# An expert's 96 rows loaded as 128 pieces of three quarters of a row, in a decoder block with 32 experts

## Chip, cores and metric

The kernel runs on one core of a Trainium2 chip, in one launch. The metric is the device time of one execution in microseconds. All tensors are float32.

## What is computed

One layer of a decoder on 1,024 tokens of 1,024 features. First come three token mixers side by side (a recurrent one, a chunked one, sliding-window attention), their gated sum and an output projection. Then comes the part that the change touches, a mixture of 32 experts of which each token uses two:

```
h = rms_norm(x, norm2_g) * (1 + sc2) + sh2
group = top-1 of softmax(h @ w_rg)              # 4 groups of 8 experts
expert 1, 2 = top-2 of softmax(h @ w_re) within the group; weights = their shares
for each expert e, on the rows of its tokens:
    gate, up = split(rows @ w_e_in[e])          # 1024 x 1024
    y = (silu(gate) * up) @ w_e_out[e]          # 512 x 1024
x = x + gt2 * (sum of each token's two y, by weight)
```

## The kernel before

The engines each run a program of their own and meet at semaphores. Only the part from the output projection on matters here.

**Router and scatter.** The output projection goes over 8 tiles of 128 tokens. For each tile VectorE (DVE) finds the two experts of a token and its rank among the tokens of that expert, and from them a place: row 96 * e + rank of a table `x_slots` in DRAM (`CAP` is 96). This is `L2262` to `L2266`; `L2266` writes the places as integers. GpSimd (POOL, `L725`) scatters the normalized rows of the tile there, once for the first and once for the second expert. Ranks of 96 and more are sent out of bounds, and handled in extra blocks of their own.

**Experts.** Then 32 experts follow, each with up to 96 rows. The work of one:

- ACT's queue loads the rows to `e_xs[s]` (`load_x`, `L1700`), two buffers in turn. The load takes 128 rows of the table, 96 of this expert and 32 of the next.
- DVE transposes them (`turn_x`, `L2386`): 12 turns of 32 partitions x 256 columns in blocks of 32 x 32, into `e_xT[s]`. ACT scales and shifts the result (`modulate`, `L1717`). Expert 0 is transposed on TensorE (PE) in place of that (`L1288`).
- PE multiplies by `w_e_in` in two halves (`step`), ACT takes the silu (`L1725`), DVE the product (`activate`, `L2368`) and its transposition (`turn_h`, `L2396`), PE multiplies by `w_e_out` (`close`), DVE scales (`y_out`, `L2377`), ACT's queue stores the rows in two pieces to `y_slots` (`L1731`, `L1732`).

The weights of an expert are three tiles of 2 MB, two of `w_e_in` and one of `w_e_out`, each 128 partitions of 16 KB that lie together in DRAM. SyncE's queue (SP) issues them when their buffer is free (`L468`, `L472`); there are two sets of buffers, and a third one that is used once, for expert 2.

The order is written out by hand. In DVE's program, one expert is `activate(e)`, `y_out(e - 1)`, `turn_h(e)`, `turn_x(e + 2)`; in ACT's it is `silu(e)`, `modulate(e + 1)`, `load_x(e + 3)`, `store(e - 1)`; in PE's `step(e)`, `close(e - 1)`. `turn_x` waits for its load (`xs0_in`, `xs1_in`), `load_x` for the turns before it on the same buffer (`xs_used`), PE's `step` for the modulated rows (`e_xT`) and for `activate` of the expert before.

At the end the rows of y are gathered per token (`L759`) and summed.

At the very start of the program ACT's queue loads 16 small vectors, the list `vec_rows`, as rows of 128 elements: `b_ada` 48 rows, two norms and `mu_a` 8 each, five vectors of 2, `conv_b_b` 4, `conv_w_b` 16, `c` 8, and four single rows of 64 elements.

Of the kernel before, what the change touches and what calls it, by code (L numbers as in the profile page):

```python
# [6 lines left out]
P = 128  # L7
# [3 lines left out]
NG, NE, TOPK, DE = 4, 32, 2, 512  # L11
CAP = 96
# [3 lines left out]
QT = 32  # L16
# [5 lines left out]
def hybrid_block(nc, I, out, dram):  # L22
    f32, i32 = mybir.dt.float32, mybir.dt.int32
    ALU, ACT, AX = mybir.AluOpType, mybir.ActivationFunctionType, mybir.AxisListType.X
    ds, ts = bass.ds, bass.ts
    x1_d, xn_d, xslot_d, yslot_d, gates_d, ga_d, mods_d = dram

    ctx = ExitStack()
    with ctx:
# [4 lines left out]
        def sem(name):  # L34
            if name not in sems:
                sems[name] = ctx.enter_context(nc.semaphore(name))
            return sems[name]
# [210 lines left out]
        def rtmp(*dims):  # L248
            n = 1
            for d in dims:  # L250
                n *= d
            v = view(r0_[0], *dims)
            r0_[0] += n
            assert r0_[0] <= TMP1 + 1056
            return v
# [3 lines left out]
        r_v, r_rank = rtmp(NT, TOPK), rtmp(NT, TOPK)  # L259
        r_m, r_em, r_t = rtmp(NT, TOPK, NE), rtmp(NE), rtmp(TOPK, NE)  # L260
        r_mem, r_pre = rtmp(2, NE), rtmp(NT, NE)
        x_m = rtmp(NT, TOPK, NE)
        r_slot, r_far = rtmp(TOPK), rtmp(TOPK)
        r_cnt, r_nx, r_cum, r_ov, r_io = (rtmp(NE) for _ in range(5))
        r_i4, r_iP, r_tok = rtmp(NG), rtmp(P), rtmp(NT)
        r_own, r_over, r_div = (rtmp(NT, TOPK) for _ in range(3))
# [15 lines left out]
        e_xs = [view(TMP0 + 2322 + D * s, D) for s in range(2)]  # L282
        e_xT = [view(TMP0 + KT * CAP * s, KT, CAP) for s in range(2)]
# [16 lines left out]
        V, A, G, E = nc.vector, nc.scalar, nc.gpsimd, nc.tensor  # L300
        TT, TS, STT = V.tensor_tensor, V.tensor_scalar, V.scalar_tensor_tensor
# [20 lines left out]
        vec_rows, n = [], 0  # L322
# [1064 lines left out]
        def _(act):  # L1387
# [47 lines left out]
            g = [0]  # L1435
# [44 lines left out]
            for t in range(NT):  # L1480
                b = bank()
# [214 lines left out]
                A.activation(v, v, ACT.Exp).then_inc(sem("r_exp"), 1)  # L1696
            act.wait_ge(sem("router_dve"), COUNTS)

            def load_x(e, s):
                act.dma_start(e_xs[s], xslot_d[ds(CAP * e, P)]).then_inc(sem(f"xs{s}_in"), 16)  # L1700

            for s in range(2):
                act.wait_ge(sem(f"x_sc{s}"), 16 * NT)
            load_x(0, 0)
            load_x(1, 1)

            def xT_out(e, s, ks=KT):
# [96 lines left out]
        def _(dve):  # L1804
# [3 lines left out]
            def link(ins):  # L1808

                chain[0] += 1  # L1810
                ins.then_inc(dsem, 1)
                dve.wait_ge(dsem, chain[0])
# [445 lines left out]
            def place(t):  # L2258

                dve.wait_ge(sem("r_rank"), t + 1)  # L2260
                rank = rank_bank(t).unsqueeze(1).to_broadcast([P, TOPK, NE])
                link(TT(r_t, r_m[:, t], rank, ALU.mult))  # L2262
                link(V.tensor_reduce(out=r_rank[:, t], in_=r_t, axis=AX, op=ALU.add))
                STT(r_slot, r_v[:, t], -float(CAP), r_rank[:, t], ALU.mult, ALU.add)
                link(TS(r_far, r_rank[:, t], float(CAP), float(8 * T), ALU.is_ge, ALU.mult))
                STT(i_dst[:, TOPK * t:TOPK * t + TOPK], r_slot, float(NE * CAP), r_far, ALU.add, ALU.add)\  # L2266
                    .then_inc(sem("x_placed"), 1)
# [111 lines left out]
            def turn_x(e, s, turn, used):  # L2379
                dve.wait_ge(sem(f"xs{s}_in"), 16 * turn + 16)  # L2380
                if used is not None:
                    dve.wait_ge(sem("win_used"), used)
                for t in range(3):
                    rows = e_xs[s][ts(t, QT), :].rearrange("p (k b n) -> p k b n", b=4, n=QT)
                    for b in range(4):
                        ins = V.transpose(e_xT[s][ts(b, QT), :, ts(t, QT)], rows[:, :, b, :])  # L2386
                ins.then_inc(sem("xs_used"), 1)

            def turn_h(e, again=True, hT=e_hT):
# [104 lines left out]
```

## Time and profile before

| | |
|---|---|
| time, median of 3 runs | 1783.63 us (1782.71 to 1785.6) |
| profiled execution, first to last instruction | 1778.4 us |
| PE busy | 1670.4 us, 94% |
| DVE busy | 1012.6 us, 57% |
| ACT busy | 442.4 us, 25% |
| POOL busy | 211.8 us, 12% |
| DMA | 363.70 MB, mean 205 GB/s |
| mean granted TensorE clock | 0.979 |

The page of a profile gives busy time by engine, then the span in 40 slices, the DMA queues, the chain of work that ended last (each step followed back to what released it), the costliest groups of instructions and the DMA issues. SyncE's and ACT's transfers go through two hardware queues (q1 and q10), GpSimd's through a software one (q0). All of them are served by the same 16 DMA engines; a queue's share is the time of its packets as a part of 16 engines' span. The profiled execution's first to last instruction is 5.2 us shorter than the median time. A busy engine isn't the bound by that alone: what counts is which wait ends last in a stage.

### The profile page before, as it was taken

What the parts mean: (1) busy time and instruction counts of PE and PEld (TensorE: products, weight loads), DVE (VectorE), ACT (ScalarE), POOL (GpSimd) and SP (SyncE); (2) the same over time, 40 slices, a digit from 0 to 9 for tenths busy, and PEclk for the clock granted to TensorE, in tenths of its full rate; (3) what the DMA queues carried; (4) which work ended last, traced back from release to release, by engine and by line L of the source; (5) the groups of instructions that cost most, each with busy time, mean ns of one, the idle gap of its engine ahead of it and who ended that gap; (6) DMA issues with size and microseconds to landing.
All of it is one profiled execution on the core that took longest, in us unless ns stands there. A gap on an engine that the chain in (4) does not pass through costs nothing.

```text
span 1778.4 us, 35422 instructions
## 1 busy us (share of the span) xinstructions
PE 1670.4 (94%) x14793; PEld 930.9 (52%) x14793; DVE 1012.6 (57%) x2453; ACT 442.4 (25%) x1072; POOL 211.8 (12%) x311
## 2 busy tenths in 40 slices
PE   5999999999999999999999999987999999999990
PEld 3455444544444545555455545545777775555550
DVE  2486526555555354443544435555778877776754
ACT  5120324333444212222122121112222122122110
POOL 3030000000110222202222051010000000000003
PEclk9999999999999999999999999988999999999995
DMA  9377218001211110101101176489899999999997
GB/s 350 120 265 252 71 71 263 25 24 32 63 48 52 47 33 16 33 21 31 34 16 33 56 292 232 148 284 370 330 425 427 426 427 426 429 427 427 429 422 303
DMA packets 109014, 363.70 MB, mean 205 GB/s; under 512 B 12890, under 2 KB 56840, under 8 KB 96428
## 3 DMA queue, kind: packets, MB, share of 16 engines
q1 hardware_dynamic: 86256, 282.70, 41.0%
q10 hardware_dynamic: 15708, 54.73, 8.4%
q0 software_dynamic: 6960, 25.04, 3.8%
q8 instruction: 60, 0.98, 0.2%
q14 instruction: 30, 0.25, 0.0%
HBM read 316.42 MB, written 58.74 MB: 211 GB/s over the span
## 4 chain that ended last, share of the span: by engine, by line
PE 80%; DMA 14%; DVE 3%; POOL 1%; issue 1%; ACT 1%; SPq 1%; ACTq 0%; POOLq 0%; DVEq 0%
PE bank L298 78%; DMA arena<-in_w_e_out 11%; DMA arena<-in_w_in 1%; POOL arena L759 1%; PE bank L945 1%; DMA arena<-y_slots,ints 1%; SPq L380 1%; DVE arena L2396 0%; DVE arena L1887 0%; PE bank L1233 0%; ACTq L1397 0%; DMA arena<-in_kn_g_c 0%; DVE arena L2386 0%; ACT arena L1523 0%; DMA x_slots<-arena,ints 0%
## 5 line engine op out<-in xcount | busy, mean ns | idle before, releaser
L298 PE MATMUL bank<-arena 128*32 128x256 f32 (+7 forms) x14414 | 1627.4, 388 | 36.4 <-DMA arena<-in_w_e_in 7.1
L298 PEld LDWEIGHTS bank<-arena 128*32 128x32 f32 (+3 forms) x14414 | 884.7, 131 | 748.5 <-issue 548.1
L2386 DVE STREAM_TRANSPOSE arena<-arena 32x256 f32<-32x256 f32 x372 | 161.9, 435 | 5.7
L2396 DVE STREAM_TRANSPOSE arena<-arena 32x128 f32<-32x128 f32 x384 | 157.5, 410 | 4.8
L1725 ACT ACTIVATE arena<-bank 128x128 f32<-128x128 f32 x96 | 19.7, 278 | 395.4 <-PE bank L298 395.4
L1717 ACT ACTIVATE arena<-arena 128x96 f32<-128x96 f32 x248 | 92.1, 460 | 5.2 <-DVE arena L2386 5.2
L2377 DVE TENSOR_TENSOR arena<-bank,arena 128x512 f32<-128x512 f32 x64 | 35.5, 557 | 99.9 <-PE bank L298 99.8
L2144 DVE TENSOR_TENSOR arena<-arena,bank 128x128 f32<-128x128 f32 (+1 forms) x40 | 11.4, 286 | 130.3 <-PE bank L298 130.3
L759 POOL DMA_INDIRECT arena<-y_slots,ints x16 | 17.1, 1070 | 542.9 <-DMA y_slots<-arena 537.9
L684 POOL TENSOR_TENSOR arena<-arena 64x256 f32<-64x256 f32 x96 | 70.2, 731 | 30.3 <-DVE arena L2120 23.7
L1887 DVE RECIPROCAL arena<-arena 128x512 f32<-128x512 f32 x10 | 33.5, 3349 | 30.8 <-ACT arena L1452 30.8
L1854 DVE SCALAR_TENSOR_TENSOR arena<-arena 128x512 f32<-128x512 f32 x56 | 42.1, 752 | 2.0
L1650 ACT ACTIVATE arena<-bank 128x128 f32<-128x128 f32 x40 | 11.1, 277 | 129.4 <-PE bank L298 129.4
L2114 DVE TENSOR_TENSOR arena<-arena,bank 128x512 f32<-128x512 f32 x32 | 21.9, 685 | 33.8 <-PE bank L298 33.3
L2368 DVE TENSOR_TENSOR arena<-arena,bank 128x128 f32<-128x128 f32 x96 | 21.8, 283 | 28.8 <-ACT arena L1725 28.1
L690 POOL TENSOR_TENSOR arena<-arena 128x512 f32<-128x512 f32 x8 | 10.2, 1270 | 232.4 <-DVE arena L2114 232.4
L1965 DVE SCALAR_TENSOR_TENSOR arena<-arena,bank 128x256 f32<-128x256 f32 x64 | 21.9, 414 | 23.8 <-PE bank L298 23.8
L1684 ACT ACTIVATE arena<-arena 128x1024 f32<-128x1024 f32 x8 | 8.5, 1057 | 104.9 <-DVE arena L2285 104.9
L1531 ACT ACTIVATE arena<-bank 128x512 f32<-128x512 f32 x16 | 9.6, 598 | 93.0 <-PE bank L298 93.0
L1523 ACT ACTIVATE arena<-arena 128x256 f32<-128x256 f32 x64 | 31.5, 493 | 0.0
L725 POOL DMA_INDIRECT x_slots<-arena,ints x16 | 15.7, 981 | 118.9 <-DVE ints L2266 94.0
L1630 ACT ACTIVATE arena<-bank 128x512 f32<-128x512 f32 x32 | 19.1, 596 | 34.7 <-PE bank L298 34.6
(337 smaller groups left out, 1030.1 us busy)
## 6 DMA issues: line engine op xcount, KB each, us to landing
arena<-in_w_e_in SPq DMA_DIRECT2D x64, 2048.0 KB, 24.4
arena<-in_w_e_out SPq DMA_DIRECT2D x32, 2048.0 KB, 25.2
arena<-in_w_ada SPq DMA_DIRECT2D x12, 2048.0 KB, 12.4
arena<-in_w_in SPq DMA_DIRECT2D x32, 512.0 KB, 3.8
arena<-x_slots ACTq DMA_DIRECT2D x32, 512.0 KB, 10.3
y_slots<-arena ACTq DMA_DIRECT2D x32, 288.0 KB, 9.3
y_slots<-arena POOLq DMA_DIRECT2D x21, 384.0 KB, 17.2
arena<-in_w_in SPq DMA_DIRECT2D x3, 2048.0 KB, 21.3
```

The lines of the kernel that those rows point to most:

```text
L298: return nc.tensor.matmul(o, l, r, start=start, stop=stop)
L684: G.tensor_tensor(a_lo[q][b], a_sm[b, :, 0, b], lvl[b, q, b].unsqueeze(1).to_broadcast([N, H, N]), ALU.mult).then_inc(sem("a_lo"), 1)
L759: pool.indirect_dma_start(out=f_y[t % 4][k], out_offset=None, in_=yslot_d, in_offset=bass.IndirectOffsetOnAxis(ap=ix[:, t:t + 1], axis=0))\
L1523: ins = A.activation(c_sc[:, j, :], c_sc[:, j, :], ACT.Exp, bias=c_nm[:, j:j + 1], accum_out=c_sum[:, j:j + 1])
L1717: ins = A.activation(e_xT[s][:, k, :], e_xT[s][:, k, :], ACT.Identity, scale=sc2e[:, k:k + 1], bias=sh2e[:, k:k + 1])
L1854: ins = STT(acc, w[:, k, :], cond[:, k:k + 1], acc, ALU.mult, ALU.add)
L1887: link(V.reciprocal(c_rs[half], c_rs[half]))
L1965: ins = STT(c_sc[:, 2 * i + a, :], dist[:, 1 if c else 0, :], -slope, PS[2 + 2 * a + i // 2][:, ts(i % 2, 2 * P)], ALU.mult, ALU.add)
L2114: TT(dst, m_sg[n % 2], PS[7], ALU.mult).then_inc(sem("m_prod"), 1)
L2377: TT(e_y[s][:, cols], PS[5 + u][:, 0:(512, 256)[u]], gt2[:, cols], ALU.mult).then_inc(sem("y_out"), 1)
L2386: ins = V.transpose(e_xT[s][ts(b, QT), :, ts(t, QT)], rows[:, :, b, :])
L2396: ins = V.transpose(hT[ts(q, QT), :, ts(t, QT)], e_h[ts(c, QT), r, :].rearrange("p (n k) -> p k n", k=4))
```

## The change

The place of a row within its expert changes. With rank r, and third = r // 32 for r under 96, the place was 96 * e + r and is now 96 * e + 3 * (r mod 32) + third, which is 3r - 95 * third. Rows i, 32 + i and 64 + i now lie together in `x_slots`, 12,288 bytes. The load takes these 12,288 bytes as four pieces of 3,072 bytes, and writes piece g of triple i to partition 32 * g + i: 128 partitions of 768 columns, 96 rows and none of the next expert's. The source is written as (4, 32, 768), the destination as (128, 768). Expert 0 is loaded as before to 96 partitions, one row each, from a source written as (3, 32, 1024).

`turn_x` puts the pieces back together: a row of 1,024 columns is cut at 768, so the quarters of the three rows lie in four groups of partitions in six parts, each turned in four instructions: 24 turns with 192, 64, 128, 128, 64 and 192 columns, where there were 12 with 256. The sum of columns is the same.

```diff
@@ -261,6 +261,7 @@
         r_mem, r_pre = rtmp(2, NE), rtmp(NT, NE)
         x_m = rtmp(NT, TOPK, NE)
         r_slot, r_far = rtmp(TOPK), rtmp(TOPK)
+        r_third = rtmp(2, TOPK)
         r_cnt, r_nx, r_cum, r_ov, r_io = (rtmp(NE) for _ in range(5))
         r_i4, r_iP, r_tok = rtmp(NG), rtmp(P), rtmp(NT)
         r_own, r_over, r_div = (rtmp(NT, TOPK) for _ in range(3))
@@ -1696,12 +1697,15 @@
                 A.activation(v, v, ACT.Exp).then_inc(sem("r_exp"), 1)
             act.wait_ge(sem("router_dve"), COUNTS)
 
+            xs_thirds = xslot_d[0:NE * CAP].rearrange("(e i a) n -> e i (a n)", e=NE, i=QT)
+
             def load_x(e, s):
-                act.dma_start(e_xs[s], xslot_d[ds(CAP * e, P)]).then_inc(sem(f"xs{s}_in"), 16)
+                act.dma_start(e_xs[s][:, 0:768], xs_thirds[ds(e, 1)].rearrange("o i (g n) -> (o g) i n", g=4))\
+                    .then_inc(sem(f"xs{s}_in"), 16)
 
             for s in range(2):
                 act.wait_ge(sem(f"x_sc{s}"), 16 * NT)
-            load_x(0, 0)
+            act.dma_start(e_xs[0][0:CAP], xslot_d[0:CAP].rearrange("(i t) n -> t i n", t=3)).then_inc(sem("xs0_in"), 16)
             load_x(1, 1)
 
             def xT_out(e, s, ks=KT):
@@ -2261,7 +2265,11 @@
                 rank = rank_bank(t).unsqueeze(1).to_broadcast([P, TOPK, NE])
                 link(TT(r_t, r_m[:, t], rank, ALU.mult))
                 link(V.tensor_reduce(out=r_rank[:, t], in_=r_t, axis=AX, op=ALU.add))
-                STT(r_slot, r_v[:, t], -float(CAP), r_rank[:, t], ALU.mult, ALU.add)
+                TS(r_third[:, 0], r_rank[:, t], float(QT), float(1 - 3 * QT), ALU.is_ge, ALU.mult)
+                link(TS(r_third[:, 1], r_rank[:, t], float(2 * QT), float(1 - 3 * QT), ALU.is_ge, ALU.mult))
+                STT(r_slot, r_v[:, t], -float(CAP), r_third[:, 0], ALU.mult, ALU.add)
+                link(STT(r_third[:, 1], r_rank[:, t], 3.0, r_third[:, 1], ALU.mult, ALU.add))
+                link(TT(r_slot, r_slot, r_third[:, 1], ALU.add))
                 link(TS(r_far, r_rank[:, t], float(CAP), float(8 * T), ALU.is_ge, ALU.mult))
                 STT(i_dst[:, TOPK * t:TOPK * t + TOPK], r_slot, float(NE * CAP), r_far, ALU.add, ALU.add)\
                     .then_inc(sem("x_placed"), 1)
@@ -2380,10 +2388,10 @@
                 dve.wait_ge(sem(f"xs{s}_in"), 16 * turn + 16)
                 if used is not None:
                     dve.wait_ge(sem("win_used"), used)
-                for t in range(3):
-                    rows = e_xs[s][ts(t, QT), :].rearrange("p (k b n) -> p k b n", b=4, n=QT)
+                for g, t, j, k0, k1 in ((0, 0, 0, 0, 6), (1, 0, 0, 6, 8), (1, 1, 1, 0, 4), (2, 1, 0, 4, 8), (2, 2, 2, 0, 2), (3, 2, 0, 2, 8)):
+                    rows = e_xs[s][ts(g, QT), 256 * j:256 * j + P * (k1 - k0)].rearrange("p (k b n) -> p k b n", b=4, n=QT)
                     for b in range(4):
-                        ins = V.transpose(e_xT[s][ts(b, QT), :, ts(t, QT)], rows[:, :, b, :])
+                        ins = V.transpose(e_xT[s][ts(b, QT), k0:k1, ts(t, QT)], rows[:, :, b, :])
                 ins.then_inc(sem("xs_used"), 1)
 
             def turn_h(e, again=True, hT=e_hT):
```

On ACT's queue, the loads of experts 0, 1 and 2 stand in these rows (destination by partitions and elements). Before:

```order
L1700 DMA arena<-x_slots 128x1024 x2
L1710 ACTIVATE arena<-bank,arena 128x96 x4
L1700 DMA arena<-x_slots 128x1024
L1717 ACTIVATE arena<-arena 128x96 x8
L1700 DMA arena<-x_slots 128x1024
```

Now:

```order
L1708 DMA arena<-x_slots 96x1x1024
L1703 DMA arena<-x_slots 128x1x768
L1714 ACTIVATE arena<-bank,arena 128x96 x4
L1703 DMA arena<-x_slots 128x1x768
L1721 ACTIVATE arena<-arena 128x96 x8
L1703 DMA arena<-x_slots 128x1x768
```

Nothing changed its place; the loads have other shapes, and the lines are other ones.

On DVE, one expert in the written-out part before the loops, from `y_out` on. Before:

```order
L2377 TENSOR_TENSOR arena<-bank,arena 128x512
L2377 TENSOR_TENSOR arena<-bank,arena 128x256
L2396 STREAM_TRANSPOSE arena<-arena 32x4x32 x12
L2386 STREAM_TRANSPOSE arena<-arena 32x8x32 x12
L2368 TENSOR_TENSOR arena<-arena,bank 128x128 x3
```

Now:

```order
L2385 TENSOR_TENSOR arena<-bank,arena 128x512
L2385 TENSOR_TENSOR arena<-bank,arena 128x256
L2404 STREAM_TRANSPOSE arena<-arena 32x4x32 x12
L2394 STREAM_TRANSPOSE arena<-arena 32x6x32 x4
L2394 STREAM_TRANSPOSE arena<-arena 32x2x32 x4
L2394 STREAM_TRANSPOSE arena<-arena 32x4x32 x8
L2394 STREAM_TRANSPOSE arena<-arena 32x2x32 x4
L2394 STREAM_TRANSPOSE arena<-arena 32x6x32 x4
L2376 TENSOR_TENSOR arena<-arena,bank 128x128 x3
```

The turns of x stand between the turns of h and the next expert's product, as before, and are 24 in five runs.

On DVE in the router, the places of one tile. Before:

```order
L2263 TENSOR_REDUCE arena<-arena 128x2
L2264 SCALAR_TENSOR_TENSOR arena<-arena 128x2
L2265 TENSOR_SCALAR arena<-arena 128x2
L2266 SCALAR_TENSOR_TENSOR ints<-arena 128x2
L2228 COPY arena<-bank 128x512
```

Now:

```order
L2267 TENSOR_REDUCE arena<-arena 128x2
L2268 TENSOR_SCALAR arena<-arena 128x2
L2269 TENSOR_SCALAR arena<-arena 128x2
L2270 SCALAR_TENSOR_TENSOR arena<-arena 128x2
L2271 SCALAR_TENSOR_TENSOR arena<-arena 128x2
L2272 TENSOR_TENSOR arena<-arena 128x2
L2273 TENSOR_SCALAR arena<-arena 128x2
L2274 SCALAR_TENSOR_TENSOR ints<-arena 128x2
L2232 COPY arena<-bank 128x512
```

One instruction became five, ahead of the one that writes the integers.

## Rows read from the trace of the kernel before

**Rows 1.** The page, slices of 44.5 us: DMA busy in tenths, and GB/s.

```profile
DMA  9377218001211110101101176489899999999997
GB/s 350 120 265 252 71 71 263 25 24 32 63 48 52 47 33 16 33 21 31 34 16 33 56 292 232 148 284 370 330 425 427 426 427 426 429 427 427 429 422 303
```

**Rows 2.** Windows: us, each engine's busy time (instructions), clock, DMA share, GB/s.

```profile
1210.00:1300.00 90.00, 86.82 (x1579) 61.56 (x1581) 65.38 (x162) 21.93 (x67) 0.00 (x0) 0.97 0.92 370
1300.00:1460.00 160.00, 158.68 (x2944) 115.53 (x2940) 123.37 (x308) 36.51 (x115) 0.00 (x0) 1.00 1.01 427
1460.00:1690.00 230.00, 218.54 (x3944) 131.78 (x3932) 170.65 (x444) 45.07 (x144) 0.00 (x0) 1.00 1.01 427
```

**Rows 3.** The chain that ended last, 1550 to 1700 us: start, us, what.

```profile
1560.68 27.93 DMA arena<-in_w_e_out
...
1588.85 5.43 PE bank L298 x96
...
1594.42 27.91 DMA arena<-in_w_e_out
```

**Rows 4.** Timeline 1300 to 1345 us: start, us, engine, line, operation.

```profile
1314.44 0.38 ACTq L1700 DMA_DIRECT2D arena<-x_slots  x1
...
1317.32 0.69 DVE L2377 TENSOR_TENSOR arena<-bank,arena 128x512 f32<-128x512 f32 x1 [2.23 <-PE bank L298]
1318.94 0.42 DVE L2377 TENSOR_TENSOR arena<-bank,arena 128x256 f32<-128x256 f32 x1 [0.93 <-PE bank L298]
...
1319.28 5.08 DVE L2396 STREAM_TRANSPOSE arena<-arena 32x128 f32<-32x128 f32 x12
...
1324.39 5.38 DVE L2386 STREAM_TRANSPOSE arena<-arena 32x256 f32<-32x256 f32 x12
...
1329.81 0.47 ACT L1717 ACTIVATE arena<-arena 128x96 f32<-128x96 f32 x1
1329.95 0.68 DVE L2368 TENSOR_TENSOR arena<-arena,bank 128x128 f32<-128x128 f32 x3 [0.18 <-ACT arena L1725]
1329.98 0.38 ACTq L1700 DMA_DIRECT2D arena<-x_slots  x1
1330.18 2.60 ACT L1717 ACTIVATE arena<-arena 128x96 f32<-128x96 f32 x7
...
1334.48 0.42 DVE L2377 TENSOR_TENSOR arena<-bank,arena 128x256 f32<-128x256 f32 x1 [0.94 <-PE bank L298]
```

**Rows 5.** DMA queues and landings (last column, median us), 1460 to 1690 us.

```profile
q1 hardware_dynamic: 5869, 85.41, 87.0%
q10 hardware_dynamic: 5103, 12.77, 14.0%
...
arena<-x_slots ACTq DMA_DIRECT2D x13, 512.0 KB, 10.3
```

**Rows 6.** DMA queue 10 from 0 to 13 us: packets, MB, share.

```profile
q10 hardware_dynamic: 196, 0.06, 2.3%
```

**Rows 7.** The chain, 1195 to 1213 us.

```profile
1201.78 3.51 DMA x_slots<-arena,ints
...
1205.39 3.33 DMA arena<-x_slots
```

**Rows 8.** Timeline of DVE, 1198.6 to 1200.2 us.

```profile
1199.28 0.16 DVE L2264 SCALAR_TENSOR_TENSOR arena<-arena 128x2 f32<-128x2 f32 x1
1199.36 0.16 DVE L2265 TENSOR_SCALAR arena<-arena 128x2 f32<-128x2 f32 x1
1199.55 0.16 DVE L2266 SCALAR_TENSOR_TENSOR ints<-arena 128x2 int32<-128x2 f32 x1
```

**Rows 9.** Groups of turns by form, 200 to 1778 us: busy, mean ns of one.

```profile
L2386 DVE STREAM_TRANSPOSE arena<-arena 32x256 f32<-32x256 f32 x372 | 161.9, 435 | 5.7
L2396 DVE STREAM_TRANSPOSE arena<-arena 32x128 f32<-32x128 f32 x384 | 157.5, 410 | 4.8
...
L2148 DVE STREAM_TRANSPOSE arena<-arena 128x128 f32<-128x128 f32 x32 | 10.0, 311 | 1.1
```

## The prediction

> **What bounds the kernel now.** I read the slices first: from about 1,250 us to the end the DMA engines move 425 to 429 GB/s in slice after slice, whatever the rest does [rows 1]. Then the windows of the expert stage: from 1300 to 1460 us the PE is busy 158.68 of 160 us and the DMA share is 1.01; from 1460 to 1690 the DMA share is still 1.01 and PE has gaps (218.54 of 230) [rows 2]. So both run at their limit first, the weights loaded ahead are used up, and after 1460 DMA alone sets the pace. The chain says the same: a `w_e_out` transfer of 27.9 us, 5.43 us of PE, the next transfer, once per two experts (1560.68 to 1594.42, 33.74 us, 16.87 us an expert) [rows 3]. An expert moves 6.29 MB of weights, 0.524 MB of x and 0.393 MB of y, 7.21 MB; at 427 GB/s that is 16.88 us. PE needs about 15.5 (two `x_slots` issues, 1314.44 and 1329.98, are 15.54 us apart) [rows 4].
>
> **What one engine has to do.** Sixteen engines share this, so I price one. In 1460 to 1690 queue 1 (weights) moved 85.41 MB in 87.0% of 16 x 230 us, 3,202 engine-us, 26.7 GB/s an engine; queue 10 (x and y) moved 12.77 MB in 14.0%, 515 engine-us, 37 us more than at 26.7, or 7 ns for each of 5,103 packets [rows 5]. A row of weights of 16 KB is then 0.614 us, a 4,096-byte row of x 0.160, a 3,072-byte piece 0.122, a 1,024-byte piece 0.045. One expert on one engine: 24 x 0.614 + 8 x 0.160 + 6 x 0.122 + 6 x 0.045 = 17.02 us, against 16.87 in the chain: within 1%.
>
> **How a load is dealt out.** The bytes of x fall by a quarter, 131 KB an expert, and if 16 engines still share the load each does 8 x 0.122 for 8 x 0.160. Whether 16 do is the question. The new load's source is written (4, 32, 768): four quarters outermost, then 32 triples of rows; its destination has 128 partitions. The old one had 128 on both sides. The trace shows at its start what a small outer count does: the 16 loads of `vec_rows` have 48, 8, 8, 8, 2 (five times), 4, 16, 8 and 1 (four times) rows, 114 pieces, and queue 10 shows 196 packets until 13 us [rows 6]. That leaves 82 packets beyond the pieces, which is exactly one each for 16+8+8+8+10+4+16+8+4 engines; 16 transfers on 16 engines would leave 256. So in this kernel a transfer is spread over as many engines as its outermost count lets it, at most 16. No row shows a transfer whose two sides differ, 4 against 128. I take it that the smaller, common count decides, since the pieces of both sides have to be paired on an engine; that is an argument and not a row, and the rivals hold the other outcome. [...]
>
> **The change, part by part.**
> - The x loads of experts 1 to 31. On four engines each engine moves 32 pieces of 3,072 bytes, 32 x 0.122 = 3.90 us, for 8 x 0.160 = 1.28: 2.62 us more an expert on these four, and weights are complete only when the slowest engine is. An expert then costs 17.02 + 2.62 = 19.6 us on them, above PE's 15.5 from the first experts on. 31 x 2.62 = 81.2 us.
> - The load of expert 0 has (3, 32, 1024) against 96: three engines, 32 x 0.160 = 5.12 us for 1.28, 3.8 us more. It is on the path: scatter 3.51 us, load 3.33, then PE [rows 7].
> - Given back: engines that stood idle. From 1210 to 1300 the mean is 370 GB/s for 427 [rows 2], 57/427 x 90 = 12.0 us in which buffers were full. With the four engines behind, their queues aren't empty there. -12.0 us.
> - The places: four more DVE instructions in a router tile (L2264 becomes five, L2265 stays). In the last tile L2264 starts at 1199.28 and L2266 at 1199.55, with steps of 0.08 us where nothing is waited for and 0.19 where the result is [rows 8]. Two of the added are issued free and three in turn: 2 x 0.08 + 3 x 0.2, less the 0.08 that goes, about 0.7 to 0.8 us before the last scatter. I take 0.8. In tiles 0 to 6 the POOL queue waits for DVE anyway while PE runs the output projection back to back; nothing there.
> - 24 turns for 12. The elements are the same. A turn of 256 columns takes 435 ns, contiguous turns of 128 columns 311 [rows 9]: 0.97 ns a column and 187 ns fixed. The new sizes (192, 64, 128, 128, 64, 192 columns, four each) come to 8 x 373 + 8 x 249 + 8 x 311 = 7.46 us, with 13 ns between them 7.8 for 5.38 [rows 4]. 2.4 us more an expert; above, 12 more at the 410 ns of L2396 are 4.9 us; below, 12 x 187 ns are 2.2. DVE works 0.69 + 0.69 + 0.42 + 5.08 + 5.38 = 12.3 us an expert [rows 4], 14.7 with this, under 19.6: nothing. If that cover were gone (a period of 15.5) it would cost: from the end of the turns (1324.39 + 5.38 = 1329.77) ACT modulates for 3.0 us, and PE ends the step before at 1334.5, where DVE takes its y [rows 4]; 1.7 us of slack against 2.4, halved because two experts are in flight, 0.35 us an expert, about 5 us until DMA binds again.
> - The x load is waited for by DVE, and behind that wait stand `activate`, `y_out` and `turn_h` of the next expert, which PE waits for. Today a load lands in 10.3 us [rows 5]: 8 pieces, each behind a 16 KB row of weights (0.160 + 0.614 = 0.774, 6.2 in all) and 4.1 us besides. With 32 pieces it is 32 x 0.736 + 4.1 = 27.7 us. It is issued 0.2 us behind the turns that free its buffer, and is wanted two experts later less the turns: 2 x 19.6 - 8 = 31.2 us. It just fits, and it fits because the period has grown; at 15.5 it would be late. So in the first experts x makes PE wait before the weights do. That costs no further time as long as the four engines are never idle, since their work is what is summed.
>
> Sum: 81.2 + 3.8 - 12.0 + 0.8 = 73.8 us. The profiled span of 1778.4 becomes about 1852; the median of the runs is 5.2 us above that span, so 1783.6 becomes 1857.4. The tail stays: the last gathers, sums and stores are not touched.
>
> **Rivals.**
> 1. *Four engines, and each piece dearer or late.* [...] Against it: the y stores, 96 rows over 16 engines, cost only 7 ns a packet more. If a piece takes twice as long, 32 x 0.122 x 31 = 121 us come on top: 1978. Half of that is 1918, which I take. [...]
> 2. *All 16 engines share the load* (the 128 partitions decide): faster. From 1280 on DMA has no slack, 25 loads (experts 7 to 31) of 131,072 bytes less at 427 GB/s, 0.307 us each, are 7.7 us; the scatter's 0.8 goes against it: 1776.7. The turns' 0.35 us an expert are hidden, because weights are short later. It decides from the point where the share of an engine is 8 pieces. For it: the destination is the same 128 partitions. Against it: the pieces of the source are counted from four.
> 3. *All 16 engines, and DVE becomes the bound.* From the y step at 1318.94 to the end of modulation (1330.18 + 2.60) are 13.8 us [rows 4], then PE's 15.5 for the expert: 29.3 for a loop that carries two experts. With turns at the upper 4.9 us it is 34.2, 17.1 an expert: 1.6 us more than 15.5 for 16 experts to 1460 and 0.2 more than 16.87 for 14 behind it, 29 us, 1813. It decides from 33.2 us a loop; with 2.4 us it is 31.7 and hidden. Against it: contiguous turns of 128 columns at 311 ns.
>
> **How the numbers follow.** Forecast 0.64, rival 1 0.17, rival 2 0.13, rival 3 0.06. Predicted 1857 us, the forecast's own range 1838 to 1882 (the idle 12 us not used or all early waits absorbed; the loads late by a few us an expert). The range for all is 1805 to 1940: nearly all of the forecast, half of rival 1, most of rival 3; about 0.79. A change under 0.2% (3.6 us) can't be told from none. Slower: the forecast, rival 1, most of rival 3, 0.85; same: 0.03; faster: rival 2, 0.12.
>
> **What would show it.** In the profile after: landing of the x loads at 25 to 30 us for 10.3; queue 10 with 12 packets fewer for each of 31 loads and 13 for the first, 385 fewer in all, at 4 MB less; DMA share in the expert stage about 0.85 with GB/s near 360, since 12 engines idle; PE gaps of about 4 us in every expert at a wait for DVE or ACT, with 19 to 20 us between two `x_slots` issues; 24 turns in 7 to 8 us. Wrong: landings near 10 us and an unchanged number of packets (rival 2); a period above 21 us (rival 1); a DVE without idle time (rival 3).

## The result and the profile after

| | before | after |
|---|---|---|
| time, median | 1783.3 us (1782.7 to 1785.6) | 1941.2 us (1935.1 to 1950.6, 4 runs) |
| ratio, 95% interval | | 1.089 (1.0857 to 1.0923) |
| profiled execution, first to last instruction | 1778.4 us | 1945.3 us |

The change costs 158 us; 74 were forecast. The profiled execution of after is 167 us above that of before, 9 more than the medians differ; windows and chains below are of it.

The page of after: span, the slices (48.6 us each; DMA busy in tenths), queue 10, the chain by line, two groups of instructions.

```profile
span 1945.3 us, 35826 instructions
...
DMA  9485072102120111011117546769888897988867
GB/s 332 140 289 184 22 253 64 33 22 54 55 73 17 31 31 31 14 30 31 31 44 278 224 161 222 279 251 390 294 324 328 313 374 278 394 309 333 348 237 274
...
q10 hardware_dynamic: 15291, 50.53, 7.2%
...
PE bank L299 61%; DMA arena<-x_slots 19%; DVE arena L2394 6%; DVE arena L2404 2%; DMA x_slots<-arena,ints 1%; POOL arena L760 1%; PE bank L946 1%; DMA arena<-in_w_ada 1%; DMA arena<-y_slots,ints 1%; ACT arena L1721 1%; DVE arena L1891 0%; ACTq L1398 0%; DMA arena<-in_kn_g_c 0%; PE bank L810 0%; PE bank L1234 0%
...
L2394 DVE STREAM_TRANSPOSE arena<-arena 32x192 f32<-32x192 f32 (+1 forms) x744 | 225.1, 303 | 165.1 <-DMA arena<-x_slots 155.0
...
L1721 ACT ACTIVATE arena<-arena 128x96 f32<-128x96 f32 x248 | 92.2, 455 | 175.7 <-DVE arena L2394 175.7
```

The level line of 425 to 429 GB/s [rows 1] is gone. The chain waits for loads of x in place of weights: 19% of the span. Queue 10 had 15,708 packets and has 15,291, which is 417 fewer: 31 x 12 + 13 for the engines that no longer take part, as forecast, and 32 for rows. Those 32 I had missed: expert 0's load took 128 rows before, and the text on the change has it as 96.

The windows that answer to [rows 2], and one to the end of the stage:

```profile
1210.00:1300.00 90.00, 60.51 (x959) 39.60 (x963) 49.66 (x163) 13.77 (x40) 1.94 (x2) 0.81 0.68 238
1300.00:1460.00 160.00, 122.88 (x2137) 72.03 (x2129) 102.71 (x312) 28.58 (x88) 0.00 (x0) 0.89 0.88 336
1460.00:1690.00 230.00, 191.27 (x3380) 111.91 (x3384) 160.71 (x484) 39.95 (x124) 0.00 (x0) 0.91 0.87 336
1690.00:1880.00 190.00, 141.04 (x2440) 79.92 (x2436) 127.32 (x394) 31.55 (x96) 0.00 (x0) 0.87 0.87 336
```

336 GB/s from 1300 to the end, at a DMA share of 0.87 or 0.88, and PE idle for a sixth to a quarter of the time. The share is near the forecast's 0.85, the rate is below its 360. The granted clock falls to 0.87 with the gaps. PE waits for others here, so I take the clock as a consequence; no run separates what it costs.

The chain of after, answering to [rows 7] and going on (start, us, what):

```profile
1162.23 17.84 DMA x_slots<-arena,ints
...
1215.10 3.51 DMA x_slots<-arena,ints
1218.71 0.90 ACTq L1708
1219.64 13.73 DMA arena<-x_slots
...
1241.03 38.90 DMA arena<-x_slots
...
1319.90 32.19 DMA arena<-x_slots
...
1359.88 36.12 DMA arena<-x_slots
...
1403.81 42.99 DMA arena<-x_slots
```

The stage starts 13.3 us later (first load issued at 1218.7, before at 1205.4), and loads of x are links of the chain: 13.7 us for expert 1's (issued at 1219.64), then 32 to 43 us in these lines and up to 46.7 us later on. Such a link lasts from the load's issue to its landing. Expert 0's load is issued at 1218.71, and PE, which waits for it, starts at 1227.88, 9.2 us later; before, these were 1205.39 and 1208.85, 3.5 us. In the timeline of after:

```profile
1227.88 1.51 PE L1289 MATMUL bank<-arena 96*128 96x96 f32 x8 [15.64 <-DMA arena<-x_slots]
```

From the issue of expert 4's load (1267.4) to that of expert 31's (1828.5) it is 20.8 us an expert; before it was 16.2 (1236.1 to 1673.1).

In some stretches of after, nothing but loads of x moves. Queue 10 from 1545 to 1549 us, where queue 1 has no packet, and two windows:

```profile
q10 hardware_dynamic: 161, 0.41, 26.0%
...
1451.00:1462.00 11.00, 1.64 (x16) 0.91 (x20) 9.96 (x36) 2.97 (x8) 0.00 (x0) 0.50 0.25 100
1464.00:1468.00 4.00, 4.00 (x84) 2.49 (x76) 3.85 (x11) 0.00 (x0) 0.00 (x0) 1.00 0.01 4
```

A quarter of the 16 engines works, four, and from 1451 to 1462 us PE waits meanwhile (1.64 us busy of 11). From 1464 to 1468 even the four are idle. Laying the trace's packet records over one another from 1300 to 1800 us, I find fewer than four engines at work for 1.4% of the time. So four engines are busy nearly all the time, and the other twelve wait for them.

How such a link stops the engines, in the timeline of after at 1403 us (in brackets: us idle before it, released by):

```profile
1403.81 0.57 ACTq L1703 DMA_DIRECT2D arena<-x_slots  x1
...
1414.25 7.57 DVE L2394 STREAM_TRANSPOSE arena<-arena 32x192 f32<-32x192 f32 x24 [4.07 <-DMA arena<-x_slots]
...
1421.86 0.47 ACT L1721 ACTIVATE arena<-arena 128x96 f32<-128x96 f32 x1 [3.95 <-DVE arena L2394]
...
1424.89 17.43 PE L299 MATMUL bank<-arena 128*32 128x256 f32 x288 [2.48 <-ACT arena L1721]
```

DVE waits for the load, ACT for DVE, PE for ACT. The 24 turns take 7.57 us; their three forms (busy, mean ns) cost what was forecast from [rows 9], a few per cent less:

```profile
L2394 DVE STREAM_TRANSPOSE arena<-arena 32x192 f32<-32x192 f32 x248 | 91.9, 370 | 158.3 <-DMA arena<-x_slots 155.0
L2394 DVE STREAM_TRANSPOSE arena<-arena 32x128 f32<-32x128 f32 x248 | 74.9, 302 | 3.4
L2394 DVE STREAM_TRANSPOSE arena<-arena 32x64 f32<-32x64 f32 x248 | 58.3, 235 | 3.4
```

And the queues of after in 1460 to 1690 us, which answer to [rows 5]:

```profile
q1 hardware_dynamic: 4700, 68.65, 77.1%
q10 hardware_dynamic: 3884, 8.56, 10.4%
```

This pair of numbers holds most of what the forecast lacked. Queue 1 moved 68.65 MB in 0.771 x 3,680 (16 x 230) engine-us: 24.2 GB/s an engine, where it was 26.7. A row of weights, which the change doesn't touch, takes 0.677 us on average in place of 0.614.

### The profile page after: what moved, and what is told of

Same layout as the page of the kernel before. It is cut to its first block, busy times and chain, and to the rows that moved or that the text cites. A ratio compares the mean times of both kernels' runs of the same rounds, so it can differ in the third digit from the quotient of the medians.

```text
span 1945.3 us, 35826 instructions
## 1 busy us (share of the span) xinstructions
PE 1702.2 (88%) x14793; PEld 909.5 (47%) x14793; DVE 1076.8 (55%) x2857; ACT 445.6 (23%) x1072; POOL 212.3 (11%) x311
## 3 DMA queue, kind: packets, MB, share of 16 engines
q10 hardware_dynamic: 15291, 50.53, 7.2%
## 4 chain that ended last, share of the span: by engine, by line
PE 63%; DMA 22%; DVE 10%; issue 2%; ACT 1%; POOL 1%; ACTq 1%; DVEq 0%; POOLq 0%; SPq 0%
PE bank L299 61%; DMA arena<-x_slots 19%; DVE arena L2394 6%; DVE arena L2404 2%; DMA x_slots<-arena,ints 1%; POOL arena L760 1%; PE bank L946 1%; DMA arena<-in_w_ada 1%; DMA arena<-y_slots,ints 1%; ACT arena L1721 1%; DVE arena L1891 0%; ACTq L1398 0%; DMA arena<-in_kn_g_c 0%; PE bank L810 0%; PE bank L1234 0%
## 5 line engine op out<-in xcount | busy, mean ns | idle before, releaser
L299 PE MATMUL bank<-arena 128*32 128x256 f32 (+7 forms) x14414 | 1658.9, 398 | 159.6 <-ACT arena L1721 97.2
L299 PEld LDWEIGHTS bank<-arena 128*32 128x32 f32 (+3 forms) x14414 | 863.1, 134 | 924.7 <-issue 612.3
L2394 DVE STREAM_TRANSPOSE arena<-arena 32x192 f32<-32x192 f32 (+1 forms) x744 | 225.1, 303 | 165.1 <-DMA arena<-x_slots 155.0
L2148 DVE TENSOR_TENSOR arena<-arena,bank 128x128 f32<-128x128 f32 (+1 forms) x40 | 11.4, 286 | 130.3 <-PE bank L299 130.3
L1631 ACT ACTIVATE arena<-bank 128x512 f32<-128x512 f32 x32 | 19.1, 596 | 34.7 <-PE bank L299 34.6
## 6 DMA issues: line engine op xcount, KB each, us to landing
arena<-in_w_ada SPq DMA_DIRECT2D x12, 2048.0 KB, 12.5
```

The costliest lines, as they stand in the source:

```text
L299: return nc.tensor.matmul(o, l, r, start=start, stop=stop)
L2394: ins = V.transpose(e_xT[s][ts(b, QT), k0:k1, ts(t, QT)], rows[:, :, b, :])
```

## The experiments

Of each, the time is the median and the ratio is to the kernel before in the same comparison, with its 95% interval; differences in us are to that kernel's median there (1783.2 to 1783.8 us). Of each edit the main lines are shown, without the semaphore increments and waits that go with them.

**One transfer of four, made as four.** Changed kernel; the source of each quarter is 32 rows, so each of the four transfers has 32 on both sides.

```diff
-                act.dma_start(e_xs[s][:, 0:768], xs_thirds[ds(e, 1)].rearrange("o i (g n) -> (o g) i n", g=4))
+                for g in range(4):
+                    act.dma_start(e_xs[s][ts(g, QT), 0:768], xs_thirds[ds(e, 1), :, ts(g, 768)].rearrange("o i n -> (o i) n"))
```

> The changed kernel with each x load of experts 1 to 31 written as four transfers, one for each quarter, 32 rows of source to 32 partitions: outermost counts 32 and 32. Places, 24 turns and bytes are those of the change. If the spread over four engines is the cause, the x loads land in 8 to 14 us, an expert takes 16.6 us again and the time is 1770 to 1795. If the small pieces or the turns are the cause, it stays above 1900.

1841.3 us, 1.0326 (1.0295 to 1.0357): neither of the two outcomes that I expected. 100 of the 158 us go, 58 stay. Its window:

```profile
1460.00:1690.00 230.00, 197.04 (x3516) 119.54 (x3508) 175.11 (x541) 42.53 (x132) 0.00 (x0) 1.00 1.01 381
```

All 16 engines are busy again (share 1.01), and yet they move 381 GB/s, not 427. So the number of engines is one cause, and there is a second.

**The outermost count alone.** The kernel before; x load with the same 128 rows in the same 128 pieces, source written with 2, 4, 8 or 16 outermost (the rows of an expert then come in another order).

```diff
-                act.dma_start(e_xs[s], xslot_d[ds(CAP * e, P)])
+                act.dma_start(e_xs[s], xslot_d[ds(CAP * e, P)].rearrange("(i g) n -> g i n", g=G))   # G = 2, 4, 8, 16; not for expert 0
```

> The kernel before with only the source of the x load written as (4, 32, 1024) for experts 1 to 31, the same 128 rows in another order (the rows of an expert reach other partitions than they should, so the output is another one). Bytes, places and the 12 turns are those of before. If the outermost count of the source decides on how many engines carry the load, each of four moves 32 x 4,096 bytes, 3.84 us more an expert than before, and the time is 1900 to 2050. If the destination's 128 decide, it is 1783.

> The kernel before with the source of the x load written as (16, 8, 1024) for experts 1 to 31: the same 128 rows of 4,096 bytes in another order (so the output is another one), eight neighbouring partitions on each of 16 engines. No engine has more than before. If only the number of engines matters: 1783. If it costs to write partitions that are another engine's in the weight transfers, as the longer weight rows in the traces of split4 and rows96 suggest, queue 1 moves under 26 GB/s an engine and the time is 1800 to 1850.

> As perm16, with (8, 16, 1024): eight engines with 16 rows of 4,096 bytes each, 1.28 us more an expert on them. By the spread: between perm16 and perm4 (1976), 1840 to 1890. If four engines and under are a case of their own: as perm16.

> As perm16, with (2, 64, 1024): two engines with 64 rows of 4,096 bytes each, 10.2 us for 1.3, so 24 x 0.614 + 10.2 + 1 = 26 us an expert: 31 x 9 = 279 us more less 12, about 2050, by the sum over the busiest engine; with every load 64 x 0.774 = 50 us long and two buffers, up to 2300.

| outermost | time, us | ratio (95%) | packets of queue 10 |
|---|---|---|---|
| plain | 1783.3 | | 15,708 |
| 16 | 1835.3 | 1.0290 (1.0273 to 1.0307) | 15,708 |
| 8 | 1901.0 | 1.0663 (1.0642 to 1.0684) | 15,460 |
| 4 | 1976.2 | 1.1056 (1.1015 to 1.1097) | 15,336 |
| 2 | 2105.3 | 1.1808 (1.1785 to 1.1832) | 15,274 |

The packets fall by 31 x 8, 31 x 12 and 31 x 14: the engines are as many as the source's outermost count, though the destination has 128 partitions. That was "an argument and not a row" in the prediction; it is a row now. The packet records show the number directly. From 1300 to 1800 us exactly 8, 4 and 2 engines are at work for 8%, 15% and 29% of the time, and fewer for under 1% of it.

And 16 groups, with no engine missing, cost 52 us:

```profile
1460.00:1690.00 230.00, 202.18 (x3480) 118.48 (x3484) 149.80 (x395) 41.47 (x132) 0.00 (x0) 0.96 1.01 382
...
q1 hardware_dynamic: 5258, 76.58, 87.3%
```

This average hides two states. First before and then 16 groups, each in a window in which a load of x moves; then 16 groups in a window with no load of x, but with y stores:

```profile
1559.00:1564.00 5.00, 5.00 (x96) 3.37 (x92) 3.96 (x10) 0.00 (x0) 0.00 (x0) 1.00 1.00 419
...
1567.00:1573.00 6.00, 5.95 (x108) 3.74 (x100) 5.21 (x13) 0.00 (x0) 0.00 (x0) 1.00 1.00 300
1576.00:1586.00 10.00, 10.00 (x160) 5.67 (x156) 3.04 (x9) 3.29 (x11) 0.00 (x0) 0.83 1.01 429
```

The queues of the run with 16 groups in these two windows, 1567 to 1573 and 1576 to 1586 us:

```profile
q1 hardware_dynamic: 98, 1.41, 78.4%
q10 hardware_dynamic: 95, 0.39, 21.5%
...
q1 hardware_dynamic: 275, 4.00, 93.4%
```

All engines are busy in both. While the x load is in flight they move 300 GB/s in place of 419, and once it has landed 429. A row of weights takes 0.87 us beside the load and 0.61 us without it; a row of x takes 0.22 us, where before it was 0.16. So the two transfers slow one another only while both are under way, and the y stores, which read SBUF and write DRAM, slow nothing.

**Which of its two sides makes the 16 groups dear: reading or writing?** First 16 groups whose rows follow one another; the groups are 9 rows apart, so that the form stays.

```diff
+                src = xslot_d[ds(CAP * e, 9 * 16)].rearrange("(g i) n -> g i n", g=16)[:, 0:8]
```

> The kernel before; only the source of the x load of experts 1 to 31 is written as 16 groups of 8 consecutive rows, the groups 9 rows apart (the buffer is made 32 rows longer), so that 16 engines each read 8 rows that follow one another and write 8 partitions that follow one another. 128 pieces of 4,096 bytes as before. It leaves the right rows in place only for the first group of an expert. Theory A (what costs is which engine writes which partition): as in the run with 16 groups of permuted rows, 1835 us +- 8, x4 rate of the stage about 382 GB/s. Theory B (what cost there was the reading of rows 16 apart): 1783 to 1790 us, 427 GB/s.

1836.5 us, 1.0300 (1.0285 to 1.0316): theory A. The order of reading is not it. Then the same rows as two loads of 64, and, as its control, as two loads of 512 columns.

```diff
+                    for a in range(2):    # halves64
+                        act.dma_start(e_xs[s][ds(64 * a, 64)], xslot_d[ds(CAP * e + 64 * a, 64)])
+                    for a in range(2):    # cols2
+                        act.dma_start(e_xs[s][:, ts(a, 512)], xslot_d[ds(CAP * e, P), ts(a, 512)])
```

> The kernel before; the x load of experts 1 to 31 is made as two transfers of 64 rows into 64 partitions each. Same rows, bytes and 128 pieces. Theory A (the price goes with the share of pieces that another engine writes than in the one plain transfer): less than the 52 us of the 16 groups, about 35: 1818 us, 400 GB/s. Theory B (any form but the plain one costs the whole): 1835 us, 382 GB/s. Theory C (only permuted or thirds-strided rows cost): 1783 to 1788 us. [...]

> The kernel before; the x load of experts 1 to 31 is made as two plain transfers of 128 rows and 512 columns each: same rows, same bytes, 256 pieces of 2,048 bytes, still one row a partition over all 128. Theory A (what costs in the two transfers of 64 rows is which engine writes which partition, and not that there are two): 1783 to 1790 us, 425 GB/s. Theory B (two transfers in place of one cost): 1795 us and above.

1847.6 us, 1.0360 (1.0343 to 1.0377), and 1798.7 us, 1.0095 (1.0073 to 1.0117). The control came out as its theory B, 15 us dearer, but not by the rate of the transfers, which is 425 GB/s from 1460 to 1690. Its x loads, now 256 pieces, land 23.4 us after their issue in that window, and DVE waits 40.7 us for them in the stage. The loads of 64 rows land after 12.7 us and DVE doesn't wait for them, so the control's 15 us can't be taken off their 64. Their stage runs at 374 GB/s for 382 with 16 groups, so they pay at least the whole price of those, not the two thirds of it (35 of 52 us) that I expected. Whether the price goes with the share of pieces that another engine writes these runs don't tell, since no trace shows which engine writes a piece. Queue 1 in the same stretch, first the two loads of 512 columns:

```profile
q1 hardware_dynamic: 5862, 85.38, 87.1%
```

and the two loads of 64 rows:

```profile
q1 hardware_dynamic: 5161, 75.19, 87.2%
```

**96 rows, one a partition.** The kernel before, which then reads no rows of the next expert.

```diff
-                act.dma_start(e_xs[s], xslot_d[ds(CAP * e, P)])
+                act.dma_start(e_xs[s][0:CAP], xslot_d[ds(CAP * e, CAP)])
```

> The kernel before, with the x load cut to the 96 rows of the expert on 96 partitions; nothing else changed. The same bytes as the change, outermost counts 96 and 96. If bytes alone count, 25 loads of 131,072 bytes less at 427 GB/s: 1776. If it matters that only 96 partitions are written: between 1776 and 1790.

1810.6 us, 1.0155 (1.0138 to 1.0172): above both expected outcomes, and slower with a quarter fewer bytes of x.

```profile
1460.00:1690.00 230.00, 206.01 (x3680) 124.76 (x3676) 157.46 (x412) 44.93 (x143) 0.00 (x0) 1.00 1.01 395
...
q1 hardware_dynamic: 5554, 80.79, 88.8%
```

**The changed kernel with a plain load**, 128 pieces that follow one another on both sides (the quarters come to other partitions than the turns think). Then the same with expert 0's load plain as well.

```diff
+                act.dma_start(e_xs[s][:, 0:768], xslot_d[ds(CAP * e, CAP)].rearrange("r n -> (r n)").rearrange("(p n) -> p n", p=P))
```

> The changed kernel with the x loads of experts 1 to 31 written as the expert's 384 KB in a row, (128, 768) on both sides: the same 128 pieces of 3,072 bytes, but piece g of triple i in partition 4i + g, which the turns do not expect (so the output is another one). Places, 24 turns, bytes are the change's. If the cost lies in how the load is dealt to engines and partitions, the stage runs at 427 GB/s again, x lands in about 9 us, and the time is before's less 7.7 for the bytes, plus what places (9.4) and turns (3.6) showed: 1783 to 1792. If small pieces or 24 turns carry it: above 1830.

> The changed kernel with the plain 128 x 768 load of experts 1 to 31 (1801.7 us when run before), and now with expert 0's load plain too, 128 rows in 128 pieces of 4,096 bytes, in place of 96 rows on 3 engines. Rows of x come in another order than the changed kernel has them. Theory A (the load on 3 engines lands 6.2 us later, 9.53 against 3.3 us, on the chain that starts the expert stage): 1795.5 us. Theory B (something else bounds the start there): 1801 us.

1801.7 us, 1.0107 (1.0091 to 1.0122), and 1794.6 us, 1.0064 (1.005 to 1.0078). The first is 10 us above what I expected, the second is theory A. The form of the load of experts 1 to 31 alone is 139 of the 158 us, that of expert 0's load 7.1 by the medians, though the second kernel's executions range from 1788.5 to 1796.4. The first of the two, in the window and in queue 1:

```profile
1460.00:1690.00 230.00, 222.57 (x4098) 135.49 (x4092) 204.38 (x627) 50.24 (x154) 0.00 (x0) 1.00 1.01 427
...
q1 hardware_dynamic: 5975, 86.92, 88.6%
```

**Fewer bytes alone.** The kernel before with this plain load and its 12 turns.

> The kernel before; only the x load of experts 1 to 31 takes 128 pieces of 3,072 bytes (the 96 rows in one run, plain on both sides) into the first 768 columns; the 12 turns are left as they are and turn what lies there, so the values are not those of x. Theory A (the stage's transfers are full, a quarter fewer x bytes end it sooner by 31 x 0.131 MB / 427 GB/s = 9.5 us at most): 1774 to 1777 us, ratio 0.996. Theory B (a piece of 3,072 bytes costs an engine nearly what one of 4,096 costs): 1783 us, ratio 1.000.

1775.2 us, 0.9958 (0.9943 to 0.9972): theory A, 8.1 us gained.

**The places alone.** The kernel before with the changed kernel's four more instructions a tile; their result isn't used.

```diff
+                TS(r_third[:, 0], r_rank[:, t], float(QT), float(1 - 3 * QT), ALU.is_ge, ALU.mult)
+                link(TS(r_third[:, 1], r_rank[:, t], float(2 * QT), float(1 - 3 * QT), ALU.is_ge, ALU.mult))
                 STT(r_slot, r_v[:, t], -float(CAP), r_rank[:, t], ALU.mult, ALU.add)
+                link(STT(r_third[:, 1], r_rank[:, t], 3.0, r_third[:, 1], ALU.mult, ALU.add))
+                link(TT(r_third[:, 0], r_slot, r_third[:, 1], ALU.add))
```

> The kernel before with the change's four more DVE instructions in each router tile, their result not used. By the step of the prediction: 0.8 us, 1784. By the rival, that the later scatter of tile 5 meets the two slow stores of sh2 and sc2 (as the trace after shows, landing 17.8 us after its issue): 8 to 13 us before the first x load, part of which DMA's slack takes up, 1786 to 1797.

1793.1 us, 1.0057 (1.004 to 1.0073): 9.4 us, where 0.8 was forecast. The view of tile `x_slots` from 1080 to 1222 us shows the scatters (first and last start) and who waited for them (us, times). Before:

```profile
L725 POOL DMA_INDIRECT x_slots<-arena,ints x16: 970/972/1086, 1090.6 to 1201.8; - x16
...
  DVE arena L2281: 1.3, 1
```

With the places:

```profile
L726 POOL DMA_INDIRECT x_slots<-arena,ints x16: 971/973/1089, 1093.4 to 1212.2; - x16
...
  DVE arena L2286: 10.0, 3
```

From first to last scatter it is 118.8 us for 111.2. DVE writes the next tile's rows into one of two buffers that a scatter still reads, and waits for it 10.0 us for 1.3. The instructions go in front of every scatter, and this loop had no room for them. How under a microsecond of instructions becomes 8.7 us of waiting is not settled; two scatters that land after 11.2 and 10.3 us are links of the chain there, where before none but the last is. The first scatter is 2.8 us later as well, but that is not of the places: in the other versions with the places of before (those with the stores moved apart) it starts anywhere from 1090.8 to 1094.1 us.

**Two small stores moved.** In the trace two stores, together 2,048 elements of 4 bytes, are issued beside those scatters. They go ahead of the output projection here, first in the kernel before, then with the places.

```diff
-            for n, v in enumerate((sh2, sc2)):      # in SP's program, behind the router's x tiles
-                sp.dma_start(mods_d[n].rearrange("(k p) -> p k", p=P), v, ...)
+            # the same two stores right behind the wait for part_st
```

> The kernel before with the two stores of sh2 and sc2, 2,048 pieces of 4 bytes, issued before the output projection in place of among the router tiles; values and result as before. If they delay the scatters beside them: 1 to 3 us faster, 1780 to 1782. If they cost nothing today: 1783.

> The kernel before with the four more place instructions of a tile (alone 1793.1 us) and with the two stores of 2,048 elements of 4 bytes issued ahead of the output projection (alone 1789.7 us). Theory A (the tile-5 scatter is late in the run with the places because its queue stands behind those small stores): not above 1793 us, the first x load issued near 1215 us. Theory B (the two costs are of their own): 1799 us, first x load near 1225 us.

1789.7 us, 1.0035 (1.0021 to 1.0049): a miss, slower and not faster; its first scatter starts at 1100.5, 6 to 10 us later than in any version without this move, so the stores hold up what they stand before. With the places 1794.2 us, 1.0063 (1.0043 to 1.0083), as with the places alone and between the two expected outcomes: the wait for the scatters falls to 5.9 us, and the late start eats the gain. That the stores lengthen the scatters' landing is not borne out: the longest landing is 12.5 us with them moved and 11.2 with the places alone. What makes one scatter land so late stays open.

**24 turns alone.** The kernel before, each of its 12 turns cut in two.

> The kernel before with only its 12 turns cut to the 24 of the change (192, 64, 128, 128, 64, 192 columns); load, places and result are those of before. By the prediction hidden in the end: 24 turns in 7.4 to 7.8 us, PE waits up to 0.4 us an expert until 1460 and less later, 1783 to 1786. If DVE's time binds: 1795 to 1815.

1786.9 us, 1.0027 (1.0015 to 1.004): 3.6 us, 0.9 us above the expected range. Nothing was forecast in the sum, and 5 for the case without cover. That case is this kernel's until 1460 us: from 1300 to 1460 PE is busy 154.47 of 160 us, for 158.68 before.

**A version with plain loads that needs no other places.** 16 turns put the quarters right. Not all of its values are the reference's, for a reason that stays open; its work and transfers are in full.

> A version of the change that keeps the partition order of a plain load: the expert's 384 KB as (128, 768), 16 turns that write each quarter to its place, rows of y found at 32 (r mod 3) + r div 3, computed once beside the experts' work; the router is that of before. By bytes: 25 x 0.307 = 7.7 us faster, 1774 to 1778. If the strided turns bind DVE (16 at over 0.45 us): 1780 to 1790.

> quarters and mods together: 1771 to 1777 if both gain, and their sum if they are independent.

1801.4 us, 1.0101 (1.0086 to 1.0117), and with the stores moved 1808.1 us, 1.0142 (1.0127 to 1.0158). No win, against an expected gain: DVE is busy 210.18 of 230 us from 1460 to 1690 (before 170.65), since a turn with strided columns takes 519 ns, 16 of them 8.3 us for the 5.4 of before, and these turns are 22% of the chain from 1300 to 1700. No version that computes the reference beats the kernel before; the 8.1 us for the bytes are there, and each way of putting the quarters back cost more.

## Why the prediction was wrong

The first mechanism was the forecast's: the source's count of 4 puts a load on four engines, and their work sets the pace. A second one was missing: while a load in this form is in flight, the weights' rows take longer. So the size was off by a factor of two. What sets it is one sum for one engine, 24 rows of weights, its pieces of x, its share of y, with the price of a row read from queue 1 of each run (16,384 bytes over MB per engine-us) and 7 ns a packet for queue 10, as in the prediction. The row's price is the mean over all 16 engines and over moments with and without a load of x. Where all 16 engines are busy the sum only restates the measured rate; what tests it are the runs with 2, 4 and 8 engines and the changed kernel.

| x load | row of weights, us | engine sum, us an expert | 31 x excess, less 12 | measured |
|---|---|---|---|---|
| before | 0.614 | 17.0 | | |
| two of 512 columns | 0.615 | 17.1 | | 15 |
| 96 rows | 0.663 | 18.0 | 19 | 27 |
| 16 groups | 0.687 | 19.0 | 51 | 52 |
| 16 groups, rows in order | 0.690 | 19.1 | 53 | 53 |
| two of 64 rows | 0.699 | 19.4 | 61 | 64 |
| 8 groups | 0.706 | 21.0 | 112 | 118 |
| 4 groups | 0.703 | 23.9 | 200 | 193 |
| 2 groups | 0.680 | 28.8 | 352 | 322 |
| changed kernel, plain load | 0.614 | 16.7 | | |
| changed kernel, four transfers | 0.689 | 18.7 | 50 | 40 |
| changed kernel | 0.677 | 21.6 | 140 | 139 |

The last two are set against the changed kernel with the plain load, the others against before; the 12 us are the forecast's idle time given back. The sum fits the large costs within a tenth and the small ones within 12 us, and the row of weights is the input that the forecast took as constant. The 15 us of the two loads of 512 columns it doesn't give; they come from late landings.

- *"Four engines, 2.62 us more an expert ... 81.2 us"*: this is the term that was mis-sized. With the 12 us given back it forecast 69 us over before; measured are 131 (139 over the plain load, less 8 for the bytes). The count of engines was right (the packets, and the runs with 2 to 16 groups). But the rows of weights went from 0.614 to 0.677 us on average: 24 x 0.063 = 1.5 us an expert, 47 us over 31 experts, and the dearer pieces of x and y make most of the other 15. Every load that spreads over all 128 partitions in the plain way leaves 0.614; every other form, with 2 to 16 engines, with rows in order or not, gives 0.66 to 0.71. With 16 groups the price is paid only while the load is in flight, by the rows of weights (0.87 for 0.61 us) and by the rows of x (0.22 for 0.16). That is what rival 1 said of the pieces of x; what it lacked is that the weights beside them pay too, and they are the larger part. Why the two meet is not shown. That it is a matter of which engine writes which partition, theory A in near16 and halves64, stays my guess: near16 came out at the time that theory gave, but no trace shows which partitions an engine writes.
- *"The y stores cost only 7 ns a packet more"* was held against rival 1. It is true and says nothing on it: the stores read SBUF, and the 429 GB/s with y stores and no x load in flight show that they slow nothing. What costs is the load of x, which writes SBUF: 300 GB/s with 16 groups while it is in flight.
- *"It just fits"*: the load lands in 32 to 47 us on the chain, not 27.7, and was allowed 31.2. That puts x, not weights, on the chain. It costs little beyond the engine sum, as forecast: an expert takes 20.8 us from issue to issue (21.1 by its 7.08 MB at 336 GB/s) against a sum of 21.6, and the four engines are seldom idle (fewer than four at work for 1.4% of the time).
- *"The places: 0.8"* and *"in tiles 0 to 6 ... nothing there"*: false, 9.4 us. POOL does wait for DVE there (94.0 us in 7 waits before the change), but DVE also waits for POOL's scatters through two buffers, and in that loop it waited already (1.3 us). I priced the instructions at the last tile and read only one of the two waits.
- *Expert 0's load, "3.8 us more"*: 7.1. In that pair of runs the load lands after 9.53 us on three engines and after 3.41 in the plain form, 6.1 us more and not 3.8. It isn't the load of expert 1 on four engines that adds to it: in the first of the pair that load is plain, and in after, where it is on four, the start of PE comes as late (9.2 us behind the issue). What makes the rest stays open.
- *"-12.0 given back"*: the runs with groups fit with it. In after the stretch 1210 to 1300 moved 238 GB/s, less than before, because the stage began 13 us later and waited for x. From 1283 to 1290 us next to nothing moves in after (10 GB/s at a DMA share of 0.04), the four engines included, so it was not given back in full there; how much was I can't tell apart from the rest.
- *24 turns, "nothing"*: 7.57 us as forecast, but 3.6 us of time where the period is short. That they hide in after, under the longer period, is argued and not shown.
- Fewer bytes: 8.1 us where all 16 engines share, 7.7 in rival 2.

Put together for the medians: 139.4 for the load's form, 7.1 for expert 0, 9.4 for the places, 3.6 for the turns, less 8.1: 151.4 of 157.8. The 6.4 us left are in the version with both loads plain, which is 11.4 us above before where its parts give 4.9; what they are stays open.

## What to carry to other kernels

When all DMA engines are full, price a transfer by the fullest engine (21.6 us an expert by that sum in the changed kernel, 20.8 measured), and look at the outermost count of its source before trusting its bytes: 4 put a load to 128 partitions on four engines here. Then compare its form with that of the large stream: a small load in another form than the large stream slowed the rows of the stream by two fifths while it was in flight (16 groups) and by a tenth on average, more than the bytes it saved. And before putting instructions in front of a transfer that "waits anyway", look for who waits for that transfer in turn.

## What was not expected of the hardware

- Loads of 0.39 to 0.52 MB an expert in another form slow 6.29 MB of weights by 8 to 15%: queue 1 falls from 26.7 to between 23.2 and 24.7 GB/s an engine, with the engines busy throughout (share 1.01 in the runs with 16).
- With 16 groups the rate is 300 GB/s while the load of x is in flight and 429 after it has landed, with all engines busy in both. The mean price of a row of weights hardly differs between the forms: 0.687 us with 16 groups, 0.706 with 8, 0.703 with 4, 0.680 with 2.
- With loads of 96 rows on 96 partitions, 25% smaller, the whole kernel is 1.5% slower than with 128 rows on 128.
- Two stores, together 2,048 elements of 4 bytes, moved ahead of a stage, delayed its first scatter by 6 to 10 us.
